# Moving the three slots of the rounded weights by 16, 64 and 256 bytes

## The reference, cut to what matters

```
for i in range(DEPTH):                      # DEPTH = 2
    x = layer_norm(ALPHA * x + mix, ...)    # mix: nsa_pool_mixer or gla_mixer
    x = layer_norm(ALPHA * x + sqrelu_mlp(x, mlp_w1[i], mlp_w2[i]), ...)
# then: hybrid_mixer, layer norm, hierarchical_moe, layer norm
```

## Time and profile before

| what | value |
|---|---|
| time, median of 3 runs | 1169.95 us (1168.14 to 1169.95) |
| profiled execution, span from first to last instruction | 1168.2 us |
| granted TensorE clock, mean over the span | 0.999 |
| PE busy, share of the span | 1145.9 us, 98% |
| DVE busy | 819.4 us, 70% |
| ACT busy | 625.2 us, 54% |
| DMA | 204.74 MB, mean 175 GB/s |

### The profile page before, as it was taken

One profiled execution on the slowest core, in us unless ns is written; L12 is line 12 of the kernel. 1 busy time (PEld: TensorE's weight loads), 2 busy tenths in 40 slices (PEclk: granted clock), 3 DMA queues, 4 the chain that ended last, 5 costly groups with the idle time before them and its releaser, 6 DMA issues.

```text
span 1168.2 us, 16605 instructions
## 1 busy us (share of the span) xinstructions
PE 1145.9 (98%) x6669; PEld 995.0 (85%) x6669; DVE 819.4 (70%) x1043; ACT 625.2 (54%) x783; POOL 154.3 (13%) x137
## 2 busy tenths in 40 slices
PE   8999999999999999999999999999999999999997
PEld 8988888888889888888889999989988778888775
DVE  6467876666963787666698943597267677568887
ACT  4474634433565454434456744774476326457763
POOL 8600310000410022000042040003110000000000
PEclk9999999999999999999999999999999999999999
DMA  9824565655465446655534331443156308669990
GB/s 265 194 72 145 166 228 183 202 186 189 127 200 181 137 152 221 211 180 183 195 118 166 133 108 61 153 148 125 56 177 218 129 11 278 219 219 329 358 351 36
DMA packets 138477, 204.74 MB, mean 175 GB/s; under 512 B 14131, under 2 KB 97810, under 8 KB 138402
## 3 DMA queue, kind: packets, MB, share of 16 engines
q1 hardware_dynamic: 136178, 195.79, 51.4%
q0 software_dynamic: 2224, 7.90, 2.0%
HBM read 202.63 MB, written 1.05 MB: 174 GB/s over the span
## 4 chain that ended last, share of the span: by engine, by line
PE 81%; DVE 8%; DMA 4%; SPq 3%; ACT 3%; issue 1%; DVEq 0%; ACTq 0%
PE PS L448 21%; PE PS L453 15%; PE PS L676 11%; PE PS L488 9%; PE PS L646 8%; DVE w_lo L1561 2%; PE PS L1342 2%; SPq L2994 2%; PE PS L592 2%; PE PS L1355 2%; ACT w_hi L2299 1%; DMA ring<-in_expert_w_up 1%; DVE st L1590 1%; PE PS L1267 1%; DVE res L1588 1%
## 5 line engine op out<-in xcount | busy, mean ns | idle before, releaser
L1561 DVE TENSOR_TENSOR w_lo<-ring,w_hi 128x2048 fp32r<-128x2048 f32 x169 | 399.8, 2374 | 133.5 <-ACT w_hi L2299 130.8
L2299 ACT ACTIVATE w_hi<-ring 128x2048 fp32r<-128x2048 f32 x168 | 321.1, 1914 | 167.9 <-PE PS L453 111.3
L448 PE MATMUL PS<-w_hi,o_hi 128*128 128x512 f32 x340 | 133.5, 393 | 1.8 <-DVE o_lo L1829 1.1
L448 PE MATMUL PS<-w_hi,o_lo 128*128 128x512 f32 x340 | 132.9, 391 | 0.0
L2311 ACT ACTIVATE AR<-PS 128x512 f32<-128x512 f32 x100 | 55.7, 598 | 94.9 <-PE PS L1342 38.1
L488 PE MATMUL PS<-x_both,w_hi 128*128 128x512 f32 x448 | 106.1, 389 | 0.0
L488 PEld LDWEIGHTS PS<-x_both,w_hi 128*128 128x128 f32 x448 | 84.2, 188 | 17.4
L453 PE MATMUL PS<-w_lo,o_hi 128*128 128x512 f32 x340 | 85.6, 390 | 0.0
L453 PE MATMUL PS<-x_both,w_lo 128*128 128x256 f32 x656 | 85.4, 283 | 0.2 <-DVE w_lo L1699 0.2
L453 PEld LDWEIGHTS PS<-x_both,w_lo 128*128 128x128 f32 x656 | 83.4, 192 | 2.5 <-DVE w_lo L1699 0.4
L676 PE MATMUL PS<-w_hi,x_both 128*128 128x512 f32 x320 | 84.6, 400 | 0.2 <-DVE x_both L2088 0.2
(11 more groups left out here) (506 smaller groups left out, 1998.2 us busy)
## 6 DMA issues: line engine op xcount, KB each, us to landing
ring<-in_mlp_w SPq DMA_DIRECT2D x64, 1024.0 KB, 5.4
ring<-in_w_in SPq DMA_DIRECT2D x32, 1024.0 KB, 6.6
ring<-in_c_w_in SPq DMA_DIRECT2D x12, 1024.0 KB, 5.4
ring<-in_expert_w_gate SPq DMA_DIRECT2D x24, 512.0 KB, 4.7
ring<-in_expert_w_up SPq DMA_DIRECT2D x24, 512.0 KB, 6.0
ring<-in_expert_w_down SPq DMA_DIRECT2D x11, 1024.0 KB, 6.8
ring_e<-in_expert_w_down SPq DMA_DIRECT2D x5, 1024.0 KB, 6.9
ring<-in_a_w_in SPq DMA_DIRECT2D x4, 1024.0 KB, 8.5
```

The source lines that it names most:

```text
L448: mm(out, a, b, start=first and i == 0, stop=False, skip_group_check=True)
L1561: v.tensor_tensor(w_lo[:, m % PARTS], ring_at(index[split[m]]), w_hi[:, m % PARTS].bitcast(F32), ALU.subtract)\
L2299: a(w_hi[:, m % PARTS], ring_at(index[split[m]]), ACT.Copy).then_inc(S("hi_split"), 1)
```

## The change

The two buffers become flat and 64 elements longer, and each slot becomes a slice of its own, with its start moved by 4, 16 and 64 elements: 16, 64 and 256 bytes. `w_hi[n]` and `w_lo[n]` then stand for the slots in place of `w_hi[:, n]` and `w_lo[:, n]` everywhere.

```
-        w_hi = sb("w_hi", [P, PARTS, PIECE], F32R)
-        w_lo = sb("w_lo", [P, PARTS, PIECE], F32R)
+        SLOT_AT = (4, PIECE + 16, 2 * PIECE + 64)
+        w_hi, w_lo = ([t[:, o:o + PIECE] for o in SLOT_AT]
+                      for t in (sb("w_hi", [P, PARTS * PIECE + 64], F32R), sb("w_lo", [P, PARTS * PIECE + 64], F32R)))
...
         def colview(t, n):
-            return t[:, n, :].rearrange("p (k n) -> p k n", k=KT)
+            return t[n].rearrange("p (k n) -> p k n", k=KT)
...
-                    v.tensor_tensor(w_lo[:, m % PARTS], ring_at(index[split[m]]), w_hi[:, m % PARTS].bitcast(F32), ALU.subtract)\
+                    v.tensor_tensor(w_lo[m % PARTS], ring_at(index[split[m]]), w_hi[m % PARTS].bitcast(F32), ALU.subtract)\
...
-                    a(w_hi[:, m % PARTS], ring_at(index[split[m]]), ACT.Copy).then_inc(S("hi_split"), 1)
+                    a(w_hi[m % PARTS], ring_at(index[split[m]]), ACT.Copy).then_inc(S("hi_split"), 1)
```

More of the change, by code:

```diff
@@ L358, in colview @@
         def colview(t, n):
-            return t[:, n, :].rearrange("p (k n) -> p k n", k=KT)
+            return t[n].rearrange("p (k n) -> p k n", k=KT)
         def rowview(t, n):
-            return t[:, n, :].rearrange("p (k n) -> p k n", k=2)
+            return t[n].rearrange("p (k n) -> p k n", k=2)
         def arrived(eng, name):
@@ L604, in low @@
                     return part(t, b, x_lo, w)
-                wh, wl = (w[:, n, :].rearrange("p (k n) -> p k n", k=KT // 2) for w in (w_hi, w_lo))
+                wh, wl = (w[n].rearrange("p (k n) -> p k n", k=KT // 2) for w in (w_hi, w_lo))
                 rounded(0, 0)
@@ L612, in pair_with_norm @@
                 n = take_high(names[1])
-                wh_, wl_ = (w[:, n, :].rearrange("p (k n) -> p k n", k=KT // 2) for w in (w_hi, w_lo))
+                wh_, wl_ = (w[n].rearrange("p (k n) -> p k n", k=KT // 2) for w in (w_hi, w_lo))
                 rounded(0, 1)
@@ L876, in gate_up @@
                     n = take_high(("gu", 2 * e + half))
-                wh, wl = (w[:, n, :].rearrange("p (u k n) -> p k u n", u=2, k=KT // 2) for w in (w_hi, w_lo))
+                wh, wl = (w[n].rearrange("p (u k n) -> p k u n", u=2, k=KT // 2) for w in (w_hi, w_lo))
                 tiles = tiles_of(e)
@@ L1691, in _ @@
             ve.wait_ge(S("first_weights"), 16)
-            v.tensor_copy(w_hi[:, 0, halves[0]], ring[:, 0, halves[0]]).then_inc(S("first_hi"), 1)
+            v.tensor_copy(w_hi[0][:, halves[0]], ring[:, 0, halves[0]]).then_inc(S("first_hi"), 1)
             for h in range(2):
@@ L1698, in _ @@
                 ve.wait_ge(S("hi_split" if h else "first_hi"), 1)
-                v.tensor_tensor(w_lo[:, 0, halves[h]], ring[:, 0, halves[h]], w_hi[:, 0, halves[h]].bitcast(F32), ALU.subtract)\
+                v.tensor_tensor(w_lo[0][:, halves[h]], ring[:, 0, halves[h]], w_hi[0][:, halves[h]].bitcast(F32), ALU.subtract)\
                     .then_inc(S("pieces_split" if h else "first_lo"), 1)
@@ L2197, in low_half @@
                 lo, w, r = (x.rearrange("p (u k n) -> p u k n", u=2, n=W)[:, :, 2 * h:2 * h + 2]
-                            for x in (w_lo[:, m % PARTS], w_hi[:, m % PARTS], ring_at(index[("gu", 0)])))
+                            for x in (w_lo[m % PARTS], w_hi[m % PARTS], ring_at(index[("gu", 0)])))
                 ve.wait_ge(S("hi_split" if h else "first_high"), m + 1 if h else 1)
@@ L2363, in _ @@
             arrived(act, split[0])
-            a(w_hi[:, 0, half], ring[:, 0, half], ACT.Copy).then_inc(S("hi_split"), 1)
+            a(w_hi[0][:, half], ring[:, 0, half], ACT.Copy).then_inc(S("hi_split"), 1)
             pieces[0] = 1
@@ L2702, in rounded_half @@
                 w, r = (x.rearrange("p (u k n) -> p u k n", u=2, n=W)[:, :, 2 * h:2 * h + 2]
-                        for x in (w_hi[:, part[chunk] % PARTS], ring_at(index[chunk])))
+                        for x in (w_hi[part[chunk] % PARTS], ring_at(index[chunk])))
                 a(w, r, ACT.Copy).then_inc(S("hi_split" if h else "first_high"), 1)
```

## The result

The changed kernel takes 1172.78 us, the median of four runs from 1171.71 to 1177.1, against 1169.95 for the kernel before: a ratio of 1.0034 with a 95% interval of 1.0022 to 1.0046, which is 2.6 to 5.4 us slower (the two medians alone are 2.8 us apart). The profiled execution has a span of 1171.5 us (time 1173.26) where that of before had 1168.2.

What follows compares the result with a forecast made beforehand. It took the kernel as bound by TensorE's matmul steps (98% busy). Split, moved tiles and 256 columns at 0, plus 4.7 us on 512 columns times 0.9, gave 4.3 on 1169.95: 1174.2 us, range 1157 to 1184.

Steps and rivals of the forecast that it cites:

- Split, 0: Making the two parts on ScalarE and VectorE: new slot addresses change no duration, 0 us, upper bound +0.4 us.
- Tiles behind w_lo, 0: Tiles placed behind `w_lo` move together by 512 bytes, keeping distances among themselves: 0 us.
- A distance price on 512 columns, read off `expert`: Matmuls of 512 columns pay 6 ns at another distance (397 less 391 in the experts); 2364 matmuls, a third per slot.
- Rivals that laid the 6 ns to `expert` itself or to its place: Within "Nothing happens": the price is `expert`'s own or its place's, time 1170 us; that rival's chance 0.26.
- A distance that is no multiple of 64 pays, the others don't: On 512 columns only slot 0 of both buffers pays: 788 x 6 ns, 4.7 us of TensorE's time; chance 0.34.
- the share on the path: Part of TensorE's added time that reaches the end: between 81% and 98%, taken as 90%, making 4.7 us 4.3.
- 256 columns, 0: Matmuls of 256 columns pay nothing for the new distances, 0 us; 6 ns of gain kept for a rival.
- The rival that reads collide at distance 0: Streamed and stationary reads share memory at multiples of 512 bytes, so shifts gain: 1161.5 or 1149 us; chance 0.23.
- The likeliest case by itself: Only slot 0 pays, 1174.2 us: from 1171.5 (3 ns, 81%) to 1175.4 us (7 ns, 98%).
- the rival in which all new distances pay: Only multiples of 512 bytes are free, five of six slots pay on 512 columns: 1180.6 us, up to 1183.5; chance 0.17.
- the prediction's reading of 16-byte lines and independent read ports: By the skill's rule all shifts are whole lines and cost nothing: sum 0, time 1170 us.

Runs made afterwards that it cites:

- run at −16: All slots of both buffers 16 bytes short of a multiple of 256 from x and o: 1182.02 us against 1169.74 for the kernel before, single run.
- run with 32 unused bytes: Kernel before with 32 unused bytes of SBUF ahead of `w_hi`, distances between w, x and o unchanged: 1169.64 us, ratio 1.0001.
- run at +32: All slots of both buffers 32 bytes past a multiple of 256 from x and o: 1179.43 us against 1169.74 for the kernel before, single run.
- The map: Runs with all slots at one distance from x and o, eight distances from −64 to +128 bytes with the kernel before as 0; times 1169.38 to 1182.02 us.
- run at +64: All slots of both buffers 64 bytes past a multiple of 512 from x and o: 1169.38 us, ratio 0.9998 to the kernel before.
- version by piece: Each piece's start in its slot chosen for its matmuls (64, 32 or 0 bytes), against the kernel before: 1165.69 us against 1169.56, ratio 0.9965.

## Why the prediction was right, and where it wasn't

The time was forecast at 1174.2 and is 1172.8; slower, by a term on TensorE alone. Step by step:

**Split, 0: held.** The medians of L1562 and L2300 are 2291 and 1915, against 2292 and 1915. In the run at −16, too, VectorE's and ScalarE's busy times are within 1 us of before, so these engines don't see the distance.

**Tiles behind w_lo, 0: held** for their place (the run with 32 unused bytes). As a distance it would not have been free; it was 512 bytes, and 256 is a whole period.

**A distance price on 512 columns, read off `expert`: held.** The run at +32 shows it from both sides: `expert` at distance 0 has 391, o at 32 has 395. Rivals that laid the 6 ns to `expert` itself or to its place are out. The earlier trace rows had a hint of this that was misread: with `expert` on both sides the duration is 392, so that nearly all of the 6 ns is gone and not half.

**"A distance that is no multiple of 64 pays, the others don't": failed.** This was a choice without a row under it, and it is wrong. 64 bytes cost L489 7 ns by its step and the streamed `w` 1 to 2, 2.6 us in slot 1; 16 bytes cost L489 1 ns or less while the streamed `w` moved by 4 ns, not 6. Slot 0 on 512 columns measured 2.7 us where 4.7 stood, before the share on the path. Slot 2 has the right distance and pays all the same, 1.0 us, because its stream follows slot 1's (with slot 1 back at 256, slot 2's term is 0.1); the prediction gave each matmul its own price and knew no carry-over.

**256 columns, 0: failed.** They gained 1.4 ns at 16 bytes and 4 to 5 at 64, 3.8 us together, more than half of what 512 columns lost. The prediction had a row for it, `expert` past `o_lo` at 277 beside 283, took 0 as the middle and kept the 6 ns for a rival. The rival that reads collide at distance 0 was thus right in sign for this one form, and for 512 columns the opposite holds; whether reads collide at all, no run shows.

So the nearness of 1174.2 is in part luck: +6.3 and −3.8 by slots and forms stand where +4.7 for one slot did. The share of 0.9 on the path got no test either: the span grew by more than the steps' sum, 3.3 against 2.5. What was foretold of group means came out (L489 at 392 for 391, `w_lo` past o at 391 for 392, `w_lo` past `expert` at 397) and of the timeline half did: there are steps of 232 to 234 in every third piece, but for L489 it is slot 1's.

**Sums in the prediction that do not come out.** The likeliest case by itself would start at 1171.9 (1169.95 and 1.9), not at 1171.5. In the rival in which all new distances pay, the third slot of `w_lo` was counted as a sixth of all matmuls; by the counts used there `w_lo` has 596 of the 2364 (340, 160 and 96), so that slot has 199, 2165 pay, and the rival's time is 1181.6 in place of 1180.6 (with 7 ns and 98%, 1184.8 in place of 1183.5, just over the end of the range). Neither changes the likeliest time.

**The rules weighed.** By the prediction's reading of 16-byte lines and independent read ports the sum was 0. The runs show otherwise: all distances tried are whole lines, and six of the seven other than 0 and 256 cost 6 to 12 us. What the Trainium skill's SBUF — State Buffer states ("Specifications (TRN2)" and "Who interferes with whom") is thus not enough here, as it doesn't speak of the distance between a matmul's two operands. A matmul of 512 float32r columns here takes 226.6 ns at best, and no distance brought it lower. The Trainium skill's TensorE: Matmul & The Clock Gate ("Wait — 56ns, not 53.3ns?") puts the step of back-to-back matmuls at 2.5 ns over the columns divided by 2.4 GHz, and at 215.7 ns for 512 columns. The float32r step measured here is 11 ns over that, and 13 over the 213.3 that 512 divided by 2.4 is.

**What stays open.** Why the distance matters at all: no view here shows what TensorE waits for inside a step. What chooses between 113 and 118 for 256 columns at +64; the stream ahead is part of it. The map has one trace per distance and eight points, so finer ones, or others for x, o and the weights than one for all, may be better still. And 0.8 us between the steps' sum and the spans of before and after are not placed. They are less than the runs scatter.

## What to carry to other kernels

Where TensorE sets the time, the distance between the streamed and the stationary tile, modulo 256 bytes, is a setting of its own: here float32r matmuls of 512 columns want 0 (every other distance tried costs 1 to 8 ns of 228), and of 256 columns with the moved tile stationary +64 (5 ns of 120, as long as the stream ahead allows it). Look for tiles that the allocator put at an odd offset, like `expert`, before looking at the code. Compare steps from start to start, by buffer slot and form. The total showed nothing for the run at +64, in which terms of +6 and −10 us had cancelled, and in the changed kernel the means over the slots hid that slot 1, and not only slot 0, paid. And when a price is read off one tile, take its size and sign for that form only.

## What the runs showed of the hardware that was not expected

- Where the steps in these traces settle on one value (granted clock 1.00 in the MLP, the 2.4 GHz level), the four values seen most are whole multiples of 16 clocks: 226.7 ns is 544 clocks, 233.3 is 560, 120 is 288, 113.3 is 272. At many distances it doesn't settle on one value but runs through a fixed cycle: with all slots at 64 the streamed `w` goes 225 229 232 over and over and L489 goes 231 236; with all at 16 the streamed `w` goes 234 235 230 228. The steps of 118 in the version by piece are another such cycle, of 117, 118 and 119.
- The step has a memory: L489 in slot 2 takes some ten matmuls behind another stream until it settles, L489 in slot 1 two (238 238, then 233 and 234). For 256 columns at +64 there are two end values, 113 and 118, and what ran ahead has a part in which it is.
- Distances that differ by 256 bytes gave the same steps where it was tried (256 as 0 for all slots; in the changed kernel `w_lo` at 272 and 320 has 118 and 114 with 256 columns, as at 16 and 64), and the effect is not symmetric: −16 costs the streamed `w` 8 ns, +16 costs it 4; −64 costs it 5, +64 1.
- 4 us saved on TensorE gave 0.8 of span with all slots at +64 (one execution each), with ACT's share of the chain at 6% for 3%: even at 98% busy, other work stands close behind TensorE.
